# The scan's triangular inverse in 64x64 products, and four buffers zeroed a stage earlier

## The chip, the cores and the metric

The kernel runs on one core of a Trainium2 chip. The metric is the device time of one launch in microseconds (us), as the median of three runs. The engines are named as in the profile: PE is TensorE's matmul, PEld its weight load, DVE is VectorE, ACT is ScalarE, POOL is GpSimd, SP is SyncE.

## What is computed

A decoder layer on 512 tokens of width 1024: a projection, eight heads of RWKV-7 time mixing beside eight heads of dilated window attention, an output projection, and a feed-forward stage that picks single experts by product keys. The part that matters here is the recurrence of the time mixing, per head a state of 64x64:

```python
def step(state, inp):
    r_t, w_t, k_t, v_t, a_t, b_t = inp
    sa = jnp.einsum('bhij,bhj->bhi', state, a_t)
    state = (state * w_t[:, :, None, :] + sa[..., None] * b_t[:, :, None, :]
             + v_t[..., None] * k_t[:, :, None, :])
    return state, jnp.einsum('bhij,bhj->bhi', state, r_t)
...
_, y = lax.scan(step, state0, xs)
```

## The kernel before

The program is a chain of stages, each a block in which every engine runs its own instruction list: `project`, `attend`, `prepare`, `scan`, `normalise_heads`, `mix`, `route`, `experts`. The engines meet only through semaphores: `wait_ge` holds an engine's whole list, `then_inc` counts a finished instruction. Between stages there is a meeting of all engines, and GpSimd alone clears the semaphores of the stage that ended (`next_stage`, line 167). Nothing reorders the lists: the order is the one written.

`prepare` (line 524) computes the scaled vectors of all tokens. GpSimd has two instructions there: a small one at line 606, and at line 608 a product that waits for VectorE (`s_k`).

`scan` (line 691) works through the 512 tokens in 8 chunks of 64 (C = 64), in two halves of HC = 4 chunks. Two heads share the 128 partitions: partitions 0 to 63 hold the even head of a pair, 64 to 127 the odd one (`par`). There are HP = 4 pairs. Matrices of a pair lie in block-diagonal buffers `*_bd` of shape [128, 4 chunks, 4 pairs, 128], whose off-diagonal quarters are zero. In each half:

1. VectorE copies the scaled vectors into the diagonal blocks of `bbd` and `kbd` (lines 912 to 918). In the first half this waits for GpSimd's memsets (line 741; eight buffers, counted by `s_zero`).
2. Chunk by chunk TensorE forms Gram products (lines 775 and 778); VectorE masks them into `lbd`, `rbtbd`, `aktbd`, `rktbd` (line 929) and starts the inverse in `ttbd` (line 936); GpSimd adds the identity (line 745).
3. The triangular inverse, for the four chunks together, in NL = 5 levels (lines 794 to 829). It keeps an inverse T in `tbd` and its transpose in `ttbd`. A level is: X = L^T T for each chunk (TensorE, line 814), masked into `xbd` by VectorE (line 942); the "turn", a transpose of T through PSUM (line 799), copied out by ScalarE (line 890); then the second product, `ttbd` by `xbd` (line 827), added to T by VectorE (line 948). In the last level the order of the operands is swapped, so the result is the transpose. `xbd` and `ttbd` are the memory of `bbd` and `kbd`; `tbd` lies in `mixed`. The products with L of chunk c use PSUM bank c % 2, the second products bank 2 + c % 2, and the turns bank 4 + c, so a product waits for the evacuation of the one two chunks before (`s_xbd`, `s_yadd`).
4. Chunk after chunk, a chain through the state (lines 832 to 856), whose products are made by `two_heads` (lines 197 to 203): for each pair, two products with 64 of the 128 stationary columns each, into the two halves of the output partitions (line 202).

In the second half VectorE also runs `norm_step` (line 666) of the first half's output, one step after the second addition of each level (lines 949 and 950).

## Time and profile before

| | us |
|---|---|
| median of three runs | 1902.52 (1901.14 to 1902.91) |
| the profiled execution, as a whole | 1903.89 |
| its span | 1901.9 |
| scan, about | 288 to 484 of the span |
| inverse, first half | 325.5 to 373.1 |
| inverse, second half | 417.7 to 466.6 |

The profile is of one execution. Times are microseconds from the start of the span. A row of the timeline merges equal instructions that follow each other: start, time from the first's start to the last's end, engine, line, operation, output<-inputs, shape, count, and in brackets how long the engine was idle before and who ended that. An fp32 product is two matmul records and two weight-load records, a transpose one of each. The row "PEclk" and the clock in the windows give the granted clock as a share of 2.4 GHz; 0.50 is 1.2 GHz. Matmul records overlap, so the distance between two starts is the price of a group, and not its duration.

### The profile page before, as it was taken

How to read it: one execution, taken by the hardware profiler on the slowest of the kernel's cores; microseconds unless marked ns; L12 is line 12 of the kernel's file. 1: busy time of each engine (PE TensorE's matmuls, PEld its weight loads, DVE VectorE, ACT ScalarE, POOL GpSimd, SP SyncE). 2: the span in 40 equal slices, each digit the busy share in tenths (PEclk: the TensorE clock that was granted, in tenths of full speed). 3: DMA queues.
4: the chain of work that ended last, by engine and by line, in shares of the span. 5: the costliest groups of instructions: out<-in, count | busy, mean ns of one | idle time of the engine just before them, and what ended most of it. 6: DMA issues, size and time to landing. Idle time of an engine off the chain costs nothing.

```text
span 1901.9 us, 26134 instructions
## 1 busy us (share of the span) xinstructions
PE 1726.2 (91%) x9853; PEld 1512.0 (79%) x9853; DVE 1440.0 (76%) x2785; ACT 719.8 (38%) x1060; POOL 609.4 (32%) x356
## 2 busy tenths in 40 slices
PE   8998855979579887989998999999999999999997
PEld 6875325878468776979998999999999999978886
DVE  5564686566645999979994666888888888887765
ACT  4113542222232222358885333333333333333333
POOL 0000014010003546533333223656655655631100
PEclk9999987999799988989999999999999999999999
DMA  6310000000402223435657878999999999999983
GB/s 251 94 62 1 1 0 1 2 2 2 161 30 93 87 75 102 150 96 221 228 231 276 300 237 305 340 362 358 335 385 342 361 349 356 320 357 329 317 298 126
DMA packets 124284, 377.59 MB, mean 199 GB/s; under 512 B 11648, under 2 KB 49792, under 8 KB 123136
## 3 DMA queue, kind: packets, MB, share of 16 engines
q1 hardware_dynamic: 79664, 231.44, 34.1%
q0 software_dynamic: 36864, 134.23, 19.6%
q10 hardware_dynamic: 7632, 10.26, 1.5%
q8 instruction: 78, 1.28, 0.3%
q14 instruction: 46, 0.38, 0.1%
HBM read 338.40 MB, written 37.49 MB: 198 GB/s over the span
## 4 chain that ended last, share of the span: by engine, by line
PE 43%; DVE 11%; DMA 2%; ACT 1%; issue 0%; SPq 0%; DVEq 0%; ACTq 0%
PE ps L187 14%; PE ps L189 14%; PE ps L188 14%; DVE gated_cols L1724 8%; DVE onehot_rows L1727 2%; DMA hidden_ahead_tile<-hidden_ahead 1%; DMA wq_raw<-in_u_t 1%; ACT gate_stage L1634 0%; DVE h L1794 0%; DVE h L1801 0%; DVE v_lo L1777 0%; DVE h L1747 0%; ACT onehot_rows L1622 0%; PE ps L1828 0%; SPq L1540 0%
## 5 line engine op out<-in xcount | busy, mean ns | idle before, releaser
L187 PE MATMUL ps<-v_hi,a_hi 128*128 128x512 f32 x768 | 299.3, 390 | 2.9 <-DVE a_lo L1780 2.7
L189 PE MATMUL ps<-v_hi,a_lo 128*128 128x512 f32 x768 | 299.3, 390 | 0.0
L188 PE MATMUL ps<-v_lo,a_hi 128*128 128x512 f32 x768 | 298.8, 389 | 0.0
L187 PE MATMUL ps<-xn_hi,u_hi 128*128 128x384 f32 x832 | 282.8, 340 | 13.0 <-DVE u_lo L1716 8.5
L189 PE MATMUL ps<-xn_hi,u_lo 128*128 128x384 f32 x832 | 280.3, 337 | 0.0
L188 PE MATMUL ps<-xn_lo,u_hi 128*128 128x384 f32 x832 | 280.2, 337 | 0.0
L1606 POOL DMA_INDIRECT v_selected<-in_v,expert_index x128 | 186.2, 1454 | 290.5 <-DVE h L1747 277.4
L1777 DVE TENSOR_TENSOR v_lo<-v_raw,v_hi 128x1024 fp32r<-128x1024 f32 x128 | 156.7, 1224 | 114.1 <-ACT v_hi L1692 113.2
L1597 POOL DMA_INDIRECT u_selected<-in_u_rows,expert_index x128 | 180.9, 1413 | 141.7 <-DVE hidden_selected L1734 114.4
L1687 ACT ACTIVATE hidden<-ps 128x384 f32<-128x384 f32 x76 | 37.4, 492 | 397.5 <-PE ps L189 397.5
L1229 POOL TENSOR_TENSOR wq_lo<-wq_raw,wq_hi 128x1024 fp32r<-128x1024 f32 x40 | 102.5, 2567 | 259.0 <-ACT wq_hi L1270 259.0
L1692 ACT ACTIVATE v_hi<-v_raw 128x1024 fp32r<-128x1024 f32 x128 | 134.9, 1054 | 129.0 <-PE ps L189 117.4
L187 PEld LDWEIGHTS ps<-xn_hi,u_hi 128*128 128x128 f32 x832 | 157.9, 190 | 16.6 <-DVE u_lo L1716 8.8
L187 PEld LDWEIGHTS ps<-v_hi,a_hi 128*128 128x128 f32 x768 | 144.1, 188 | 31.8 <-DVE v_lo L1777 3.5
L1747 DVE SCALAR_TENSOR_TENSOR h<-v_selected,act_selected,h 128x1024 f32<-128x1024 f32 x128 | 163.9, 1280 | 7.0 <-DMA v_selected<-in_v,expert_index 2.9
L189 PEld LDWEIGHTS ps<-v_hi,a_lo 128*128 128x128 f32 x768 | 144.1, 188 | 30.2
L188 PEld LDWEIGHTS ps<-v_lo,a_hi 128*128 128x128 f32 x768 | 144.2, 188 | 26.8
L1734 DVE CUSTOM_DVE_ANT_0 dot_products<-u_selected,xn_tok 128x1024 bf16<-128x1024 f32 x128 | 153.8, 1220 | 14.4 <-DMA u_selected<-in_u_rows,expert_index 14.2
L188 PEld LDWEIGHTS ps<-xn_lo,u_hi 128*128 128x128 f32 x832 | 157.9, 190 | 3.4
L189 PEld LDWEIGHTS ps<-xn_hi,u_lo 128*128 128x128 f32 x832 | 157.6, 189 | 0.0
L1724 DVE TENSOR_SCALAR gated_cols<-consts_late,mixed 128x128 f32<-128x128 f32 x384 | 154.2, 473 | 0.0
L187 PE MATMUL ps<-xn_hi,wq_hi 128*128 128x384 f32 (+1 forms) x320 | 121.7, 380 | 35.3 <-POOL wq_lo L1229 35.2
(303 smaller groups left out, 3269.6 us busy)
## 6 DMA issues: line engine op xcount, KB each, us to landing
wq_raw<-in_u_t SPq DMA_DIRECT2D x128, 512.0 KB, 6.6
v_raw<-in_v SPq DMA_DIRECT2D x128, 512.0 KB, 6.6
gate_matrix<-gate_stage SPq DMA_DIRECT2D x6, 4096.0 KB, 13.0
gates<-gate_matrix SPq DMA_DIRECT2D x32, 768.0 KB, 8.3
win_raw<-in_win_t SPq DMA_DIRECT2D x26, 512.0 KB, 3.6
hidden_ahead_tile<-hidden_ahead SPq DMA_DIRECT2D x52, 192.0 KB, 5.9
wq_raw<-in_wq_t SPq DMA_DIRECT2D x16, 512.0 KB, 3.3
hidden_ahead<-hidden_ahead_tile ACTq DMA_DIRECT2D x28, 192.0 KB, 4.5
```

Source lines behind the costliest of these rows:

```text
L187: nc.tensor.matmul(out, w_hi, m_hi, start=first, stop=False)
L188: nc.tensor.matmul(out, w_hi, m_lo, start=False, stop=False)
L189: return nc.tensor.matmul(out, w_lo, m_hi, start=False, stop=last)
L1229: st.do(pool.tensor_tensor(w_lo[:, n % SPL, :], raw[:, n % RQ, :], w_hi[:, n % SPL, :].bitcast(F32), ALU.subtract), s_lo)
L1597: pool.indirect_dma_start(u_sel[:, i % GB, :], None, u_rows, bass.IndirectOffsetOnAxis(S.expert[:, i:i + 1], 0)).then_inc(s_usel[i % GB], 16)
L1606: pool.indirect_dma_start(v_sel[:, k % GB, :], None, v_rows, bass.IndirectOffsetOnAxis(S.expert[:, k:k + 1], 0)).then_inc(s_vsel[k % GB], 16)
L1692: act.activation(v_hi[:, n % 2, :], v_raw[:, n % VR, :], ACT.Copy).then_inc(s_vhi, 1)
L1724: v.tensor_scalar(cols[r % R][:, q, :], S.const("iota"), tab[:, 1, tok:tok + 1], tab[:, 2, tok:tok + 1], ALU.is_equal, ALU.mult).then_inc( ...
L1727: v.tensor_tensor(rows[r % R][:, :, :], bc(S.const("iota"), 1, Q), bc(tab[:, 0, r * Q:(r + 1) * Q], 2, NKEY), ALU.is_equal).then_inc(s_row ...
L1734: v.tensor_tensor_reduce(products[:, i % 2, :], u_sel[:, i % GB, :], S.xn_tok[:, :], 1.0, 0.0, ALU.mult, ALU.add, h_sel[:, i:i + 1]).then_ ...
L1747: v.scalar_tensor_tensor(S.h[:, GT, :], v_sel[:, k % GB, :], a_sel[:, k:k + 1], S.h[:, GT, :], ALU.mult, ALU.add).then_inc(s_sum, 1)
L1777: v.tensor_tensor(v_lo[:, p, :], v_raw[:, n % VR, :], v_hi[:, p, :].bitcast(F32), ALU.subtract).then_inc(s_vlo, 1)
```

## The change

In the inverse, T and X are kept compact, as `tc` and `xc` of [128, 4 chunks, 4 pairs, 64], both in the memory of `mixed`. Every product of a pair, the turns included, is made by the new `by_head`: for each pair and each of its two heads one product with a stationary operand of 128x64 and a moving operand of 128x64, into that head's 64 output partitions. The turn is now an ordinary product with 64 columns of the identity. The PSUM results fill 256 of a bank's 512 columns, so VectorE's masks and additions are 128x256 instead of 128x512. ScalarE writes a turned chunk into the diagonal blocks of `ttbd` with two instructions on 64 partitions (level 0: one compact copy of 128x256). In the last level VectorE writes X and adds the result block by block, two instructions each. The buffers `bbd`, `kbd`, `lbd` and `rbtbd` are allocated before `prepare`, and GpSimd zeroes them there, between its two instructions; four memsets stay in `scan`, and VectorE waits there for two of them.

```diff
@@ prepare, GpSimd
             st.do(pool.tensor_scalar(omka[:, :], S.param_all("k_a"), -1.0, 1.0, ALU.mult, ALU.add), s_pd)
+            for buf in (S.bbd, S.kbd, S.lbd, S.rbtbd):
+                st.do(pool.memset(buf[:, :, :, :], 0.0))
             pool.wait_ge(s_k, 1)
@@ scan
-        tbd = S.mixed[:, 0:4, :].rearrange("p c (j t) -> p c j t", j=HP)
+        tc, xc = (S.mixed[:, 2 * i:2 * i + 2, :].rearrange("p a (b j t) -> p (a b) j t", b=2, j=HP) for i in range(2))
+        def by_head(out, lhs, rhs):
+
+            for j in range(HP):
+                for e in range(2):
+                    last = nc.tensor.matmul(out[par[e], j, :], lhs(j, par[e]), rhs(j, par[e]), start=True, stop=True)
+            return last
@@ scan, GpSimd
-            for buf in (bbd, kbd, lbd, rbtbd, aktbd, rktbd, abd, rbd):
+            for buf in (aktbd, rktbd, abd, rbd):
                 st.do(pool.memset(buf[:, :, :, :], 0.0), s_zero)
@@ scan, TensorE
                     def turn(c, src):
-                        for j in range(HP):
-                            last = nc.tensor.transpose(blocks(4 + c)[:, j, :], src[:, c, j, :], S.const("ident"))
-                        last.then_inc(s_turn, 1)
+                        by_head(half_bank(4 + c), src, lambda j, h: S.const("ident")[:, h]).then_inc(s_turn, 1)
...
-                        for j in range(HP):
-                            last = nc.tensor.matmul(blocks(c % 2)[:, j, :], lbd[:, c, j, :], tbd[:, c, j, :],
-                                                    start=True, stop=True)
-                        last.then_inc(s_x, 1)
+                        by_head(half_bank(c % 2), lambda j, h: lbd[:, c, j, h], lambda j, h: tc[:, c, j, :]).then_inc(s_x, 1)
...
+                            by_head(half_bank(2 + c % 2), lambda j, h: ttbd[:, c, j, h],
+                                    lambda j, h: xc[:, c, j, :]).then_inc(s_y, 1)
@@ scan, ScalarE
-                        st.do(act.activation((ttbd if level else tbd)[:, c].rearrange(row), S.ps[:, 4 + c, :],
-                                             ACT.Copy), s_turned)
+                        turned = half_bank(4 + c)
+                        if level == 0:
+                            st.do(act.activation(tc[:, c], turned, ACT.Copy), s_turned)
+                            continue
+                        for e in range(2):
+                            st.do(act.activation(ttbd[par[e], c, :, par[e]], turned[par[e]], ACT.Copy), s_turned)
@@ scan, VectorE
                 for i, (dst, src) in enumerate(((bbd, S.bs), (kbd, S.ks))):
-                    if not half:
-                        dve.wait_ge(s_zero, i + 1)
...
+                        if level < NL - 1:
+                            st.do(v.tensor_tensor(xc[:, c], x, bc(mask, 1, HP), ALU.mult), s_xbd)
+                            continue
+                        for e in range(2):
+                            st.do(v.tensor_tensor(xbd[par[e], c, :, par[e]], x[par[e]], bc(mask[par[e]], 1, HP),
+                                                  ALU.mult), (None, s_xbd)[e])
...
+                        if level < NL - 1:
+                            st.do(v.tensor_tensor(tc[:, c], tc[:, c], y, ALU.add), s_yadd)
+                        else:
+                            for e in range(2):
+                                to = ttbd[par[e], c, :, par[e]]
+                                st.do(v.tensor_tensor(to, to, y[par[e]], ALU.add), (None, s_yadd)[e])
```

On TensorE, in the scan's first half, from the last Gram work (`kt_bd`) over the turns of level 0 into level 1. Before (`consts_late` is the identity, `mixed` holds T, `b_bd` X and `k_bd` the transpose of T):

```order
L202 MATMUL ps<-v_chunk,kt_bd 64x64 x8
L799 MATMUL ps<-consts_late,k_bd 128x128 x16
L814 MATMUL ps<-mixed,l_bd 128x128 x16
L827 MATMUL ps<-b_bd,k_bd 128x128 x16
L814 MATMUL ps<-mixed,l_bd 128x128 x16
L799 MATMUL ps<-consts_late,mixed 128x128 x16
```

And now, at the same place:

```order
L202 MATMUL ps<-v_chunk,kt_bd 64x64 x8
L740 MATMUL ps<-consts_late,k_bd 64x64 x32
L740 MATMUL ps<-mixed,l_bd 64x64 x32
L740 MATMUL ps<-mixed,k_bd 64x64 x32
L740 MATMUL ps<-mixed,l_bd 64x64 x32
L740 MATMUL ps<-consts_late,mixed 64x64 x32
```

The sequence is the same; each step has 32 small products instead of 16 large ones, and X is read from `mixed` instead of `b_bd`.

On ScalarE, around levels 0 to 2 of the first half, before:

```order
L890 ACTIVATE mixed<-ps 128x512 x4
L897 ACTIVATE a_bd<-r_and_a 64x16x64
L890 ACTIVATE k_bd<-ps 128x512 x4
L897 ACTIVATE a_bd<-r_and_a 64x16x64
L890 ACTIVATE k_bd<-ps 128x512 x4
```

And now:

```order
L895 ACTIVATE mixed<-ps 128x256 x4
L904 ACTIVATE a_bd<-r_and_a 64x16x64
L898 ACTIVATE k_bd<-ps 64x4x64 x8
L904 ACTIVATE a_bd<-r_and_a 64x16x64
L898 ACTIVATE k_bd<-ps 64x4x64 x8
```

From level 1 on, four copies of a turned chunk have become eight, each with a quarter of the elements.

On GpSimd, from the preparation's two instructions to the scan's last memset (`b_bd`, `k_bd`, `l_bd` and `rbt_bd` are the four buffers; the 20 ISA instructions clear semaphores):

```order
 L606 TENSOR_SCALAR one_minus_k_a<-params 128x4
-L608 TENSOR_TENSOR prepare_tmp<-z_mixed 128x2048
+L608 MEMSET b_bd 128x2048
+L608 MEMSET k_bd 128x2048
+L608 MEMSET l_bd 128x2048
+L608 MEMSET rbt_bd 128x2048
+L610 TENSOR_TENSOR prepare_tmp<-z_mixed 128x2048
 L527 UNCONDITIONAL_BRANCH
 L173 ISA x20
-L737 UNCONDITIONAL_BRANCH
-L741 MEMSET b_bd 128x2048
-L741 MEMSET k_bd 128x2048
```

Four memsets have moved from behind the 20 clearing instructions to before the preparation's product.

## Rows read from the trace of the kernel before

**Rows 1.** The page, its first line: the span.

```profile
span 1901.9 us, 26134 instructions
```

**Rows 2.** Windows: stretch, length, busy time by engine, TensorE's clock, DMA share, GB/s.

```profile
325.50:373.10 47.60, 46.85 (x400) 45.25 (x400) 27.59 (x40) 14.41 (x24) 0.00 (x0) 1.00 0.00 1
373.10:390.00 16.90, 11.96 (x320) 10.30 (x320) 8.82 (x25) 1.54 (x4) 0.00 (x0) 1.00 0.01 2
417.70:466.60 48.90, 46.92 (x400) 45.24 (x400) 31.73 (x47) 16.08 (x27) 1.99 (x1) 1.00 0.01 1
```

**Rows 3.** Timeline of one level of the inverse, first half.

```profile
334.91 3.95 PE L814 MATMUL ps<-mixed,l_bd 128*128 128x128 f32 x32
...
338.70 1.91 PE L799 MATMUL ps<-consts_late,mixed 128*128 128x128 f32 x16
...
340.45 3.95 PE L827 MATMUL ps<-b_bd,k_bd 128*128 128x128 f32 x32
...
341.54 0.69 DVE L948 TENSOR_TENSOR mixed<-mixed,ps 128x512 f32<-128x512 f32 x1 [1.95 <-PE ps L827]
...
344.24 3.95 PE L814 MATMUL ps<-mixed,l_bd 128*128 128x128 f32 x32
```

**Rows 4.** Timeline of TensorE: two groups of line 202 in a row.

```profile
308.59 0.64 PE L202 MATMUL ps<-v_chunk,rkt_bd 128*64 128x64 f32 x16
309.05 0.64 PE L202 MATMUL ps<-v_chunk,kt_bd 128*64 128x64 f32 x16
```

**Rows 5.** Timeline at the start of the chain behind the inverse.

```profile
373.16 0.69 PE L202 MATMUL ps<-z_mixed,a_bd 128*64 128x64 f32 x16 [0.78 <-DVE k_bd L948]
...
373.99 0.42 DVE L966 TENSOR_TENSOR z_mixed<-ps,v_products 128x256 f32<-128x256 f32 x1 [0.89 <-PE ps L202]
374.33 0.41 DVE L968 TENSOR_TENSOR z_mixed<-z_mixed,v_products 128x256 f32<-128x256 f32 x1
...
374.47 0.69 PE L202 MATMUL ps<-z_mixed,k_bd 128*64 128x64 f32 x16 [0.16 <-DVE z_mixed L966]
```

**Rows 6.** Timeline: VectorE and ScalarE with instructions of 256 columns.

```profile
304.42 0.87 DVE L929 TENSOR_TENSOR l_bd<-ps,consts 64x256 f32<-64x256 f32 x2 [3.66 <-PE ps L778]
...
309.74 0.94 ACT L868 ACTIVATE v_products<-ps 128x256 f32<-128x256 f32 x3 [0.70 <-PE ps L202]
```

**Rows 7.** Timeline: a step of the normalisation between two additions, second half.

```profile
426.08 1.22 DVE L673 TENSOR_REDUCE y_mean<-z_mixed 128x16 f32<-128x1024 f32 x1
```

**Rows 8.** Timeline from the preparation's end to TensorE's start; last, the second half's copies.

```profile
285.26 2.48 DVE L663 TENSOR_TENSOR z_mixed<-ps,z_mixed 128x512 f32<-128x512 f32 x4
289.81 1.80 POOL L741 MEMSET b_bd<- 128x2048 f32 x1 [13.44 <-issue]
...
291.65 4.54 DVE L916 COPY b_bd<-b_scaled 64x1024 f32<-64x1024 f32 x2 [3.90 <-POOL b_bd L741]
293.30 2.35 POOL L741 MEMSET l_bd<- 128x2048 f32 x1
...
300.82 2.08 PE L775 MATMUL ps<-r_and_a,b_bd 128*128 128x128 f32 x8 [18.87 <-DVE k_bd L916]
...
390.26 1.40 DVE L916 COPY b_bd<-b_scaled 64x1024 f32<-64x1024 f32 x2
```

**Rows 9.** Timeline: VectorE's first instruction of the stage behind the scan.

```profile
484.46 1.22 DVE L673 TENSOR_REDUCE y_mean<-z_mixed 128x16 f32<-128x1024 f32 x1 [0.32 <-PEq L695]
```

**Rows 10.** Timeline: two instructions of VectorE in the preparation.

```profile
245.39 0.43 DVE L625 TENSOR_SCALAR kk_inverse<-kk_inverse 128x512 f32<-128x512 f32 x1 [2.68 <-ACT kk_inverse L589]
...
260.74 1.22 DVE L634 TENSOR_TENSOR_SCAN decay_sum<-consts,decay_rate 128x512 f32<-128x512 f32 x1 [1.87 <-ACT gate L596]
```

**Rows 11.** Timeline of TensorE: the same groups at half the clock.

```profile
321.66 1.12 PE L202 MATMUL ps<-v_chunk,akt_bd 128*64 128x64 f32 x16 [2.91 <-DVE rkt_bd L929]
322.57 1.07 PE L202 MATMUL ps<-v_chunk,rkt_bd 128*64 128x64 f32 x16
323.43 1.07 PE L202 MATMUL ps<-v_chunk,kt_bd 128*64 128x64 f32 x16
```

More of the change, by code:

```diff
@@ L699, in scan @@
         HC = NCH // 2
-        bbd = sb("b_bd", [P, HC, HP, P])
-        kbd = sb("k_bd", [P, HC, HP, P])
+        bbd, kbd, lbd, rbtbd = S.bbd, S.kbd, S.lbd, S.rbtbd
         abd = sb("a_bd", [P, HC, HP, P])
@@ L731, in scan, with half_bank @@
         row = "p j t -> p (j t)"
-        def blocks(bank):
-            return S.ps[:, bank, :].rearrange("p (j t) -> p j t", j=HP)
+        def half_bank(bank):
+            return S.ps[:, bank, 0:HP * C].rearrange("p (j t) -> p j t", j=HP)
+        def by_head(out, lhs, rhs):
[3 more added lines that the diff above has]
+            return last
         @block.gpsimd
@@ L804, in _ @@
                             pe.wait_ge(s_eye, half * HC + c + 1)
-                            turn(c, ttbd)
+                            turn(c, lambda j, h: ttbd[:, c, j, h])
                     for c in range(HC):
                         if level == 0:
-                            pe.wait_ge(s_turned, n + c + 1)
+                            pe.wait_ge(s_turned, half * HC * (2 * NL - 1) + c + 1)
                         else:
@@ L884, in _ @@
                 take_products(half * HC + HC - 1)
-                act.wait_ge(s_zero, 9)
+                act.wait_ge(s_zero, 5)
                 spread_out = [(w, dst, e) for w, dst in ((0, abd), (1, rbd)) for e in range(2)]
@@ L925, in _ @@
                                                           (aktbd, g2, 0, "strict"), (rktbd, g2, 1, "inclusive"))):
-                        if not ch:
-                            dve.wait_ge(s_zero, 3 + i)
+                        if not ch and i >= 2:
+                            dve.wait_ge(s_zero, i - 1)
                         for e in range(2):
@@ L953, in _ @@
                 if not half:
-                    dve.wait_ge(s_zero, 9)
+                    dve.wait_ge(s_zero, 5)
                 dve.wait_ge(s_prev, 3 * HC * (half + 1))
@@ L1919, in build @@
                 S.ks = sr("k_scaled", [P, HP, T])
+                S.bbd, S.kbd, S.lbd, S.rbtbd = (sr(f"{name}_bd", [P, NCH // 2, HP, P]) for name in ("b", "k", "l", "rbt"))
                 prepare(nc, S, dram)
```

24 lines of the change are left out of this document (10 added, 14 removed).

## The prediction

> **What bounds the kernel now.** I read the windows first, then the timeline of one level of the inverse, then the timelines of the places where the same kinds of instruction already run in the new shape. The profiled span is 1901.9 us [rows 1]. The two inverses, one per half of the chunks, take 47.6 us and 48.9 us of it, together 5%; TensorE is busy for 46.85 and 46.92 us of them at a granted clock of 1.00 (2.4 GHz), while VectorE is busy for 27.59 and 31.73 us and ScalarE for 14.41 and 16.08 us [rows 2]. So in this stage TensorE is the bound. The timeline of one level shows it without a hole: products with L from 334.91, turns from 338.70, second products from 340.45, the next level's from 344.24, a period of 9.33 us, and VectorE waits for TensorE before its instructions [rows 3]. A level has 4 chunks of 4 pairs of heads. Each fp32 product of 128x128 by 128x128 is two records (32 for 16 products), so a record of a product costs (344.24 - 340.45) / 32 = 118 ns, and a turn, one record, (340.45 - 338.70) / 16 = 109 ns [rows 3]. Per chunk: 0.95 us for a product, 0.44 us for a turn. Only TensorE's cost per chunk, and then whatever comes next on VectorE and ScalarE, can move the time here. Everything after the scan stays as it is and only shifts.
>
> **The change part by part.** *The price of the new products.* Each product of a pair becomes two with a stationary operand of 64 columns and a moving operand of 64. Both still contract over all 128 partitions, because the operands taken from block-diagonal buffers hold zeros in the other head's half. That is exactly the shape in which line 202 already works: 16 records (8 products) for a chunk, alternating between the two halves of the output partitions. Of three such groups back to back the second starts at 308.59 and the third at 309.05, 0.46 later: 29 ns per record [rows 4]. The new group is therefore 0.46 us for a product instead of 0.95. A turn loses its one-record form and becomes 16 records as well: 0.46 instead of 0.44. A level's TensorE work falls from 9.33 to 12 x 0.464 = 5.57 us.
>
> *What is late next.* TensorE will not reach 5.57, since each product's PSUM bank is used again two chunks later. In the chain behind the inverse the same group starts at 373.16 and VectorE takes it at 373.99, 0.83 later; the 128x256 addition lasts 0.42 and the next group of TensorE starts at 374.47, 0.06 after its end; VectorE's own pitch is 0.34 (373.99 to 374.33) [rows 5]. So the third product of a level can't start before 0.83 + 0.42 + 0.05 = 1.30 us, where TensorE would be ready at 0.93: a wait of 0.37, once for the products with L and once for the second ones. Period: 5.57 + 2 x 0.37 = 6.31 us. ScalarE now takes a turned chunk with two 64-partition copies of 256 columns. The nearest row has three 128x256 copies in 0.94 us, a pitch of 0.28 [rows 6], so 0.56 per chunk; the first of four is out 1.5 us after its turn began (0.83 + 0.28 + 0.38), before TensorE is through its four turns (1.86), and the fourth at 3.2, when its product would start at 1.86 + 1.76 = 3.6. It stays hidden; at a pitch of 0.42, half as much again, it would cost up to 2 us in a half.
>
> *One half in sum.* Four turns 1.86; level 0, whose turns these are, 6.31 - 1.86 = 4.45; levels 1 to 3, 3 x 6.31 = 18.9. In the last level the results go block by block into block-diagonal buffers, two VectorE instructions of 64x256 at a pitch of 0.44 (two in 0.87 to 0.88) [rows 6]: a bank comes free 0.44 later, the four products take 3.08 instead of 2.23, and from the level's first product to its last addition it is 3.08 + 1.86 + 2.62 + 0.83 + 0.93 = 9.3. Sum 34.6 us. The same bookkeeping with 118 and 109 ns gives 47.5 for the kernel before, where the trace has 47.6 (325.5 to 373.1), so I trust it. Saving in the first half: 13.0.
>
> *The second half.* After the second addition of levels 0 to 3 VectorE also runs one step of the first half's normalisation, 1.22 us for the long ones plus a short one or two [rows 7]. Before, much of it lay beside TensorE's work. Now VectorE comes out of it about 0.8 us after the next product has landed (0.5 for the single-instruction steps), and the third product of the next level waits for it: 0.8 + 0.5 + 0.5 + 1.0 = 2.8. So 37.4 us against 48.8 in the trace: 11.4 saved. Together the inverses give 24.4.
>
> *The zeroing.* Four of the eight memsets leave the start of the scan. There VectorE is done with the preparation at 285.26 + 2.48 = 287.74, but its first copy starts at 291.65, when GpSimd's first memset (from 289.81) is done; and each of the four copies takes 2.27 beside the memsets (the first two 4.54 together), against 0.70 in the second half (two in 1.40). The memsets beside them last 2.35 instead of 1.80. TensorE starts at 300.82 [rows 8]. In the new code the copies wait for no memset of this stage. GpSimd's first one comes late because it clears 20 semaphores first; the others don't wait for that, for where the scan ends, VectorE goes from one stage's last instruction to the next stage's first with 0.32 us of idle time [rows 9]. So: copies at 288.06, two done at 289.46, the third in flight when the memset issues at 289.81 and done at 290.2, the fourth held until the memset ends (290.2 + 1.8 = 292.0) and done at 292.5. TensorE then starts at 292.6: 8.2 us earlier. Bounds: if VectorE does wait for the semaphores to be cleared, all four copies run beside memsets, 289.9 + 0.6 + 3 x 2.28 = 297.3, and 3.4 us are saved; if nothing collides, 288.06 + 2.8 = 290.9, 9.9 saved. I take 8.2, because the idle of 0.32 is the nearest row. The four memsets that stay end about 297.9; VectorE needs the first two of them at about 296.2.
>
> *The memsets' new place.* GpSimd does them from 239.4 to about 247, and its next work is not due until 269.9. On VectorE one instruction of that stretch is of the kind that could collide, the scaling at 245.39; the most is one memset, 1.8 us. Behind it VectorE waits 1.87 us before 260.74 for the last gate from ScalarE, whose chain doesn't pass through it, so a delay of that size is gone by then [rows 10]. I take nothing; with the cover gone it would be 1.8.
>
> Sum: 13.0 + 11.4 + 8.2 = 32.6 us. The profiled execution took 1903.89 us as a whole, 2.0 around its span, and lies 1.4 above the median of 1902.52; no term depends on that difference, so I take the sum off the median: **1870 us**.
>
> **Rivals.** (a) *The start of the scan gives little, the inverse all.* VectorE is held until the clearing is over, or the collisions are worse. The row of 0.32 us speaks against it, but that row stands at the scan's end and not its start. Saving 24.4 + 3.4 or less: 1875.
>
> (b) *TensorE's narrow records don't keep 29 ns, or ScalarE or VectorE paces.* The 29 ns come from 48 records in a row at most; a half now has 960 of them. At 33 ns the same bookkeeping gives 37.6 + 39.9 us, 5.6 more; slow strided writes on ScalarE and a VectorE pitch of 0.44 for the masks would add 2 to 3. Time 1876 to 1882.
>
> (c) *The clock falls.* After 2.91 us without work TensorE ran its groups at half the clock, 16 records in 0.86 us, 53 ns each (322.57 to 323.43) [rows 11]. If the new holes kept it there all through, both inverses would take 106.9 against 96.4: 10.5 lost, 8.2 gained, 1905, no change. Against it: in the chain behind the inverse TensorE is busy 11.96 of 16.90 us, with holes of 0.6 to 0.8, and the clock stays at 1.00 [rows 2, 5]; in the new inverse the holes are 0.4.
>
> (d) *Slower.* The 29 ns are a quarter of 118 for half the columns on both sides, so the two column halves must overlap in a burst. If in a long stream they run one behind the other, a record costs half of 118, 59 ns. Then both inverses take about 117.7 us, 21.3 more, and with 8.2 back the time is 1915. It decides from 51 ns per record on: there the loss in the inverse equals the 8.2. For it speaks that no row shows more than three such groups on end; against it, that the third group lasts 0.64 us as the second does [rows 4].
>
> The Trainium skill has a rule for such a case, in "TensorE: Matmul & The Clock Gate", section "Wait — 56ns, not 53.3ns?": when the sequencer decodes in software, it spends about 62 ns on a MATMUL, and this binds once the array's work is shorter. By that rule, 62 ns per record, the inverses would take 122.7 us and the kernel 1920. The 16 records in 0.46 us [rows 4] speak against it, so it adds nothing to the chance of (d).
>
> **How the numbers follow.** The forecast, 1870, with its own range of 1865 to 1874 (copies without collision give 1868, 27 ns per record 1867, small waits up to 1874): 0.56. (a) 0.15, (b) 0.15, (c) 0.04, (d) 0.04. More than forecast, below 1865, from shorter latencies: 0.06. The range takes in the forecast, (a) and most of (b): 1864 to 1882. A measurement of this kernel can tell about 0.2%, 3.8 us, from no change: faster 0.91, same 0.04, slower 0.05.
>
> **What would show it.** In the windows each inverse should be about 35 and 37 us long with the clock at 1.00; groups of 16 records in 0.46 us; VectorE's waits short; a level's period 6.3, in the second half about 6.9. The first copy of the scan should start some 0.3 us after the preparation's last instruction, and TensorE some 4.9 us after that instruction. The prediction is wrong if the narrow records cost more than 35 ns in a stream, if the turns' ScalarE copies have a pitch over 0.4, or if the copies at the start still take 2.27 each.

## The result and the profile after

The changed kernel takes **1869.49 us** (median of four runs, 1865.54 to 1869.96), the kernel before 1902.27 in the same session: ratio 0.9824, 95% interval 0.9807 to 0.9841, so 32.8 us faster. The forecast was 1870 with a range of 1864 to 1882. The profiled execution took 1865.54 as a whole:

```profile
span 1863.7 us, 28421 instructions
```

Its windows for the two inverses answer to [rows 2] (stretch, length, then busy time of TensorE, its weight loads, VectorE, ScalarE and GpSimd, TensorE's granted clock, DMA):

```profile
314.57:350.35 35.78, 31.79 (x960) 30.02 (x960) 20.25 (x48) 17.73 (x40) 0.00 (x0) 1.00 0.01 3
...
394.55:434.19 39.64, 34.11 (x961) 32.30 (x961) 24.40 (x56) 19.34 (x42) 2.61 (x1) 0.94 0.01 4
```

47.6 us have become 35.8, and 48.9 have become 39.6. TensorE is no longer busy without a hole (31.8 of 35.8 us), and in the second half it had a granted clock of 0.94. Of [rows 3], one level of the first half:

```profile
320.92 2.42 PE L740 MATMUL ps<-mixed,l_bd 128*64 128x64 f32 x64
...
323.14 2.07 PE L740 MATMUL ps<-consts_late,mixed 128*64 128x64 f32 x64
323.85 3.19 ACT L898 ACTIVATE k_bd<-ps 64x256 f32<-64x256 f32 x8 [5.82 <-PE ps L740]
325.01 2.81 PE L740 MATMUL ps<-mixed,k_bd 128*64 128x64 f32 x64
...
327.62 2.43 PE L740 MATMUL ps<-mixed,l_bd 128*64 128x64 f32 x64
```

The period is 6.70 us (forecast 6.31): products with L 2.22 (forecast 2.23), turns 1.87 for 64 records, 29 ns a record (1.86), second products 2.61 (2.23). The row between them explains the last: ScalarE's eight copies take 3.19 us, a pitch of (3.19 - 0.38) / 7 = 0.40. In the last level, where VectorE writes block by block, one sees TensorE wait for all three reasons in turn:

```profile
341.04 1.13 PE L740 MATMUL ps<-mixed,l_bd 128*64 128x64 f32 x32
...
342.77 0.69 PE L740 MATMUL ps<-mixed,l_bd 128*64 128x64 f32 x16 [0.59 <-DVE b_bd L953]
...
347.75 0.69 PE L740 MATMUL ps<-k_bd,b_bd 128*64 128x64 f32 x16 [0.52 <-ACT k_bd L898]
...
350.35 0.69 PE L202 MATMUL ps<-z_mixed,a_bd 128*64 128x64 f32 x16 [1.02 <-DVE k_bd L963]
```

A bank that VectorE has not freed (342.77), ScalarE's copy (347.75), and the last addition (350.35).

The start of the scan, answering to [rows 8]:

```profile
283.59 1.28 DVE L665 TENSOR_TENSOR z_mixed<-ps,z_mixed 128x512 f32<-128x512 f32 x2
285.18 1.41 DVE L921 COPY b_bd<-b_scaled 64x1024 f32<-64x1024 f32 x2 [0.32 <-PEq L527]
286.62 2.98 DVE L921 COPY k_bd<-k_scaled 64x1024 f32<-64x1024 f32 x2
286.93 2.12 POOL L747 MEMSET akt_bd<- 128x2048 f32 x1 [13.44 <-issue]
289.00 2.35 POOL L747 MEMSET rkt_bd<- 128x2048 f32 x1
289.65 2.08 PE L781 MATMUL ps<-r_and_a,b_bd 128*128 128x128 f32 x8 [9.40 <-DVE k_bd L921]
```

The copies begin 0.32 us after the preparation's last instruction (284.87) and TensorE 4.79 after it; before, 3.91 and 13.08. Three copies run alone and the fourth is held by the first memset, just as forecast.

The second half begins like this:

```profile
394.55 3.68 PE L740 MATMUL ps<-consts_late,k_bd 128*64 128x64 f32 x64 [1.03 <-ACT v_products L871]
...
402.35 1.22 DVE L675 TENSOR_REDUCE y_mean<-z_mixed 128x16 f32<-128x1024 f32 x1
402.95 1.13 PE L740 MATMUL ps<-mixed,l_bd 128*64 128x64 f32 x32
...
404.91 1.15 PE L740 MATMUL ps<-mixed,l_bd 128*64 128x64 f32 x32 [0.83 <-DVE mixed L950]
```

64 records of the turns take 3.68 us where the first half's take 2.08: here TensorE ran at half its clock. Further down VectorE's normalisation step (402.35) holds the third product at 404.91 by 0.83.

In the preparation the four memsets lie where they were meant to, and one instruction meets them:

```profile
243.25 1.79 POOL L608 MEMSET rbt_bd<- 128x2048 f32 x1
244.11 1.22 DVE L627 TENSOR_SCALAR kk_inverse<-kk_inverse 128x512 f32<-128x512 f32 x1 [2.68 <-ACT kk_inverse L589]
```

1.22 us in place of the 0.43 of [rows 10]. Of these 0.8 us 0.1 are left at the end of the preparation, as the next experiments show.

**The ledger of the profiled executions.** From the span's start to the second chain's first instruction it is 466.67 us before and 434.19 after. Stage by stage, each read as the distance between two starts in the timeline (us):

| stage | before | after | forecast saving | saving |
|---|---|---|---|---|
| ahead of the preparation | 238.45 | 237.17 | 0 | 1.28 |
| preparation | 49.29 | 47.69 | 0 | 1.60 |
| its end to TensorE's start | 13.08 | 4.79 | 8.2 | 8.29 |
| Gram stage, first half | 24.71 | 24.92 | 0 | -0.21 |
| inverse, first half | 47.63 | 35.78 | 13.0 | 11.85 |
| chain and Gram stage, second half | 44.62 | 44.20 | 0 | 0.42 |
| inverse, second half | 48.89 | 39.64 | 11.4 | 9.25 |
| everything behind | 1435.2 | 1429.5 | 0 | 5.7 |

The stages that the change touches give 8.29 + 11.85 + 9.25 = 29.4 of the forecast 32.6. The other 8.8 us of this pair of executions lie in stages on which the forecast put nothing; what the runs say of them follows.

### The profile page after: what moved, and what is told of

The parts are those of the page before. It is cut to its first block, busy times and chain, and to the rows that moved or that the text cites. A ratio compares the mean times of both kernels' runs of the same rounds, so it can differ in the third digit from the quotient of the medians.

```text
span 1863.7 us, 28421 instructions
## 1 busy us (share of the span) xinstructions
PE 1694.3 (91%) x10973; PEld 1481.2 (79%) x10973; DVE 1421.8 (76%) x2801; ACT 728.1 (39%) x1092; POOL 606.8 (33%) x356
## 4 chain that ended last, share of the span: by engine, by line
PE 45%; DVE 11%; DMA 1%; issue 0%; ACT 0%; POOL 0%; SPq 0%; DVEq 0%; ACTq 0%
PE ps L187 15%; PE ps L189 15%; PE ps L188 15%; DVE gated_cols L1739 8%; DVE onehot_rows L1742 2%; DMA gates<-gate_matrix 1%; DMA hidden_ahead_tile<-hidden_ahead 1%; PE ps L1843 0%; DVE h L1809 0%; DVE h L1816 0%; POOL u_lo L1605 0%; DVE v_lo L1792 0%; ACT v_hi L1707 0%; ACT u_hi L1632 0%; ACT o_ss L1673 0%
## 5 line engine op out<-in xcount | busy, mean ns | idle before, releaser
L1702 ACT ACTIVATE hidden<-ps 128x384 f32<-128x384 f32 x76 | 37.4, 492 | 380.0 <-PE ps L189 374.6
```

Of the source, the lines that this page charges most:

```text
L1702: act.activation(act_g[:, n % 2, :], S.ps[:, (NMID + n) % 2, 0:TD], ACT.Gelu).then_inc(s_gelu, 1)
```

## Experiments

All are edits of the changed kernel, but for the first, which is the kernel before with one part of the change. The two parts apart come first. A ratio is that to the kernel before in the same session; the changed kernel's is 0.9824 (0.9807 to 0.9841).

**e1: the zeroing alone.** The inverse stays in 128x128 products.

```diff
+            for buf in (S.bbd, S.kbd, S.lbd, S.rbtbd):      # in prepare, before wait_ge(s_k, 1)
+                st.do(pool.memset(buf[:, :, :, :], 0.0))
-            for buf in (bbd, kbd, lbd, rbtbd, aktbd, rktbd, abd, rbd):
+            for buf in (aktbd, rktbd, abd, rbd):
```

> The kernel before with one part of the change: the four buffers are allocated and zeroed in the preparation, the inverse stays in 128x128 products. Theory A (the parts act alone and add up): VectorE's first copy in the scan starts 0.3 us after the preparation's last instruction, TensorE about 4.8 us after it instead of 13.1; the time falls by 8.3 us, to 1894. Theory B (the 3 to 4 us of the gain that neither the inverse nor the scan's start shows in the trace belong to the move of the memsets, through the preparation's timing): the time falls by 11 to 12 us, and the preparation itself is 1.6 us shorter in the trace each time.

**e2: the inverse alone.** The eight memsets and their waits stay in the scan.

```diff
-            for buf in (S.bbd, S.kbd, S.lbd, S.rbtbd):
-                st.do(pool.memset(buf[:, :, :, :], 0.0))
-            for buf in (aktbd, rktbd, abd, rbd):
+            for buf in (bbd, kbd, lbd, rbtbd, aktbd, rktbd, abd, rbd):
```

> The changed kernel with all eight memsets in the scan again, and VectorE waiting for them; the inverse in 64x64 products. Theory A: the scan's start is as slow as before (TensorE 13.1 us after the preparation's last instruction), the inverses take 35.8 and 37.6 to 39.6 us, the time is 8.3 us above the changed kernel, about 1878. Theory B: 1881, and a preparation as long as in the kernel before (49.3 us).

Measured: e1 1894.13 us against 1901.28 (ratio 0.9958, 0.9942 to 0.9975), e2 1878.15 (0.9874, 0.9857 to 0.9890). So 7.2 and 23.1 us; together 30.3, against 32.8 for both at once, within the spread of some 2 us that each median has. In the trace of e1 TensorE starts 4.79 us after the preparation's end, in that of e2 13.08. Rival (a), a start that gives 3.4 or less, is out.

Of the preparation they tell more than of its memsets. It lasts 47.70 us in e1 and 47.69 in the changed kernel, both with the memsets; but also 47.58 in e2, without them, and 49.23 and 49.25 in e4 and e5 below, with them. So it has two lengths 1.6 us apart, and which one comes does not go by the memsets. It goes by TensorE's clock. In the five long ones (the kernel before, e4, e5, e7, e12) some products of the preparation ran at half clock after TensorE had waited 2.07 us, as here in the kernel before:

```profile
249.47 1.92 PE L567 MATMUL ps<-z_mixed,up_weights 128*128 128x512 f32 x2
```

In the eight short ones the same products ran at full clock behind the same wait (1.02 us at 248.16 in the changed kernel). The collision of 0.8 us costs 0.1, 47.69 against 47.58, and the 1.6 of the ledger are no saving of the change.

And e1 shows what the half clock is worth, in the old 128x128 shape, with not one instruction of the inverse changed. Its timeline at the first inverse's start:

```profile
312.24 0.69 PE L202 MATMUL ps<-v_chunk,akt_bd 128*64 128x64 f32 x16 [2.70 <-DVE rkt_bd L926]
312.75 0.64 PE L202 MATMUL ps<-v_chunk,rkt_bd 128*64 128x64 f32 x16
313.22 0.99 PE L202 MATMUL ps<-v_chunk,kt_bd 128*64 128x64 f32 x16
...
315.24 3.67 PE L798 MATMUL ps<-consts_late,k_bd 128*128 128x128 f32 x16 [1.03 <-ACT v_products L867]
```

The turns take 3.67 us where they took 1.97, and this inverse lasts 49.97 us against 47.63 before: 2.3 us from a clock that fell between two groups (0.64, then 0.99), after TensorE had waited 2.70 us.

**e3: half of ScalarE's copies.** Only the even heads' turned blocks are copied, so the odd heads' part of the inverse is left out; TensorE's and VectorE's instructions all stay.

```diff
-                        for e in range(2):
-                            st.do(act.activation(ttbd[par[e], c, :, par[e]], turned[par[e]], ACT.Copy), s_turned)
+                        st.do(act.activation(ttbd[par[0], c, :, par[0]], turned[par[0]], ACT.Copy), s_turned)
```

> The changed kernel with one of ScalarE's two copies of each turned chunk left out in levels 1 to 4 (the odd heads' blocks of the transposed inverse are not refreshed, so part of the output is not computed). Theory A (ScalarE's copies, 0.80 us per chunk, set when the second products may start, and cost 0.4 us per level): a level falls from 6.70 to 6.31 us, the first half's inverse from 35.8 to about 34.4. Theory C (the 0.4 us come from TensorE itself, narrow records with other operands being slower, or from VectorE): the level stays at 6.7.

Measured: 1866.45 us (one run). The level shows the cause:

```profile
331.90 1.78 ACT L896 ACTIVATE k_bd<-ps 64x256 f32<-64x256 f32 x4 [3.46 <-PE ps L740]
333.07 2.42 PE L740 MATMUL ps<-mixed,k_bd 128*64 128x64 f32 x64
```

The next level's products start at 335.29: with four copies the second products take 2.22 us, what the sum had (2.23), where with eight of them they take 2.61 (325.01 to 327.62). The level start to start is 6.32, where the changed kernel has 6.70 and the forecast 6.31. ScalarE's pace is the missing 0.4 us of a level. The first inverse as a whole took 37.17 us, since it began at half clock; for the same reason one can't read the gain from its length.

**e4: four banks.** Each chunk's products get a bank of their own (PSUM banks 0 to 3 for both kinds), and the two waits for VectorE two chunks back go.

```diff
-                        if n + c >= 2:
-                            pe.wait_ge(s_xbd, n + c - 1)
-                        by_head(half_bank(c % 2), lambda j, h: lbd[:, c, j, h], lambda j, h: tc[:, c, j, :]).then_inc(s_x, 1)
+                        by_head(half_bank(c), lambda j, h: lbd[:, c, j, h], lambda j, h: tc[:, c, j, :]).then_inc(s_x, 1)
```

> The changed kernel with four PSUM banks instead of two for each kind of product: chunk c uses bank c for the product with L and again for the second one, so no product waits for the evacuation two chunks before. Theory A (bank waits of 0.37 us stand once in the products with L, and the second products are paced by ScalarE): the products with L take 1.86 us instead of 2.22, the second ones stay near 2.6, a level takes 6.35 instead of 6.70, the last level gains another 0.5 to 1, the time falls by 3 to 4 us against the changed kernel. Theory C (TensorE's own pace for the stream is the limit): no change.

Measured: 1865.44 us (0.9809, 0.9792 to 0.9826). Timeline of a level of the first half:

```profile
330.64 2.09 PE L740 MATMUL ps<-mixed,l_bd 128*64 128x64 f32 x64
...
332.51 2.09 PE L740 MATMUL ps<-consts_late,mixed 128*64 128x64 f32 x64
333.23 3.20 ACT L894 ACTIVATE k_bd<-ps 64x256 f32<-64x256 f32 x8 [2.20 <-PE ps L740]
334.38 2.89 PE L740 MATMUL ps<-mixed,k_bd 128*64 128x64 f32 x64
...
337.06 1.16 PE L740 MATMUL ps<-mixed,l_bd 128*64 128x64 f32 x33
```

Products with L now take 1.87 us, no more than the turns, so the bank wait was worth 0.35 (forecast 0.37). The second products still take 2.68: there two waits lie over each other, the bank's and ScalarE's, and ScalarE's ends last. So taking the bank's away alone gives nothing there, while e3, which took ScalarE's away, gave 0.39 and left the bank's. The second half's inverse falls most, to 34.06 us against 37.75 at full clock with two banks (e11). Its levels 2 and 3 take 6.40, as in the first half, since VectorE's normalisation steps then no longer hold a bank that TensorE wants; level 1 still takes 7.04. The median can't be told from the changed kernel's.

**e5: the scan's memsets held back** until VectorE's first four copies are done.

```diff
+            pool.wait_ge(s_bd, 4)
             for buf in (aktbd, rktbd, abd, rbd):
```

> The changed kernel; GpSimd starts the scan's four memsets only when VectorE's four copies are done. Theory A (a copy that meets a memset waits for it, nothing else slows the copies): all four copies take 0.71 us, TensorE starts 3.2 us after the preparation's last instruction instead of 4.8, the time falls by 1.6 us against the changed kernel, to 1868. Theory D (the copies' wait is hidden, since VectorE later waits for the held memsets instead): TensorE starts earlier, but the first turn of the first half does not.

Measured: 1867.07 us (0.9809, 0.9794 to 0.9824). The timeline:

```profile
287.80 1.41 DVE L922 COPY b_bd<-b_scaled 64x1024 f32<-64x1024 f32 x2 [0.32 <-PEq L527]
289.24 1.41 DVE L922 COPY k_bd<-k_scaled 64x1024 f32<-64x1024 f32 x2
290.70 0.58 PE L782 MATMUL ps<-r_and_a,b_bd 128*128 128x128 f32 x1 [7.78 <-DVE k_bd L922]
290.71 1.80 POOL L748 MEMSET akt_bd<- 128x2048 f32 x1 [14.60 <-DVE k_bd L922]
```

Each of the four copies takes 0.70, the memset waits, and TensorE starts 3.22 us after the preparation's end in place of 4.79. So the held fourth copy was worth 1.57 us, what the sum put on it (292.5 against 290.9). In the median that cannot be told from nothing.

**e6: the normalisation step ahead of the level's additions**, where VectorE waits for ScalarE and TensorE anyway.

```diff
-                        if half and c == 1 and level < NL - 1:
-                            norm_step(S, dve, v, st, level, 0)
+                    if half and level < NL - 1:       # before the loop of the additions
+                        norm_step(S, dve, v, st, level, 0)
```

> The changed kernel; the normalisation step of levels 0 to 3 of the second half stands before the first addition of the level, where VectorE waits 1.9 us for TensorE, instead of after the second. Theory A (the steps delay the masks and with them the third product of the next level): the levels of the second half become as long as those of the first, 6.7 us instead of 7.4, 7.0 and 6.8, the second inverse is 1.8 us shorter, the time 1868. Theory C (the second half is longer only because TensorE started it at the half clock): the levels keep their length.

Measured: 1867.70 us (0.9822, 0.9806 to 0.9839). Start to start levels 1 to 3 of the second half are 6.71, 6.87 and 6.70 us, where the changed kernel has 7.40, 7.02 and 6.75, and the last level 9.31 in place of 10.07: 1.65 us won. But level 0 has no copies to wait for, so there the step only delays the additions, and turns and level 0 take 9.58 in place of 8.40. Of 1.65 us 0.47 stay, and the time can't be told from the changed kernel's. (e12 has four banks as well.)

**e7: Gram evictions by half of the partitions.** VectorE writes the four blocks of the even heads and then the four of the odd heads, in place of both halves of each buffer in turn. The same eight instructions.

```diff
-                    for i, (dst, src, w, m) in enumerate(outs):
-                        for e in range(2):
+                    for e in range(2):
+                        for i, (dst, src, w, m) in enumerate(outs):
```

> The changed kernel; VectorE writes the Gram products of a chunk first for the even heads (four instructions on partitions 0 to 63) and then for the odd ones, instead of alternating. Theory E (two instructions in a row on different halves of the partitions don't overlap, hence the pitch of 0.45 us against 0.34 for those on all partitions): within a group the pitch falls to 0.34, a chunk takes 3.9 us instead of 4.5, unless TensorE is then the bound at 4.2; the time falls by 2 to 5 us. Theory F (any instruction on 64 partitions, or with this access pattern, has this pitch): no change.

Measured: 1863.04 us (0.9792, 0.9777 to 0.9807).

```profile
295.46 0.42 DVE L935 TENSOR_TENSOR l_bd<-ps,consts 64x256 f32<-64x256 f32 x1 [3.88 <-PE ps L784]
295.80 0.41 DVE L935 TENSOR_TENSOR rbt_bd<-ps,consts 64x256 f32<-64x256 f32 x1
296.13 0.40 DVE L935 TENSOR_TENSOR akt_bd<-ps,consts 64x256 f32<-64x256 f32 x1
296.46 0.41 DVE L935 TENSOR_TENSOR rkt_bd<-ps,consts 64x256 f32<-64x256 f32 x1
296.90 0.43 DVE L935 TENSOR_TENSOR l_bd<-ps,consts 64x256 f32<-64x256 f32 x1
```

The first four starts are 0.34, 0.33 and 0.33 apart; the fifth, where the half changes, 0.44. In the order of before every step changed the half, at 0.45 each. A chunk takes 3.8 us in place of 4.5, the Gram stage 21.5 in place of 24.9, of which 1.2 are the clock (e11 below: 23.7 with the old order at full clock). And in both halves the inverse began at full clock. The expectation had 2 to 5 us for all this; the medians lie 6.4 apart, across two sessions.

**e10: ScalarE's two copies in alternating order.** If a change of the half costs VectorE 0.1 us, it may cost ScalarE as much.

```diff
-                        for e in range(2):
+                        for e in (1, 0) if c % 2 else (0, 1):
```

> The changed kernel with one edit: ScalarE's two copies of a turned block (one for the even heads, to partitions 0 to 63, one for the odd heads, to partitions 64 to 127) come in the order even, odd for chunks 0 and 2 and odd, even for chunks 1 and 3. So three of the seven steps from one copy to the next stay within one half of the partitions; before, all seven changed the half. Theory: the pitch of 0.40 us belongs to steps that change the half, as on VectorE, where steps within a half took 0.33 to 0.34 and steps between halves 0.44 when only its order was changed. Then steps within a half take 0.28 to 0.30, the eight copies 2.85 us in place of 3.19, the second products of a level 2.3 in place of 2.6, and a level start to start 6.4 in place of 6.7; four levels of two halves give 2 to 3 us, 1867 at most. Rival: 0.40 us is what any copy of 64 partitions takes on ScalarE when the copies come from four PSUM banks; then all pitches stay at 0.40 and the time is that of the changed kernel, 1869.

Measured: 1865.66 us (0.9817, 0.9800 to 0.9833).

```profile
328.66 2.43 PE L740 MATMUL ps<-mixed,l_bd 128*64 128x64 f32 x64
...
331.59 2.80 ACT L898 ACTIVATE k_bd<-ps 64x256 f32<-64x256 f32 x8 [2.44 <-PE ps L740]
...
334.97 2.43 PE L740 MATMUL ps<-mixed,l_bd 128*64 128x64 f32 x64
```

Eight copies take 2.80 us in place of 3.19. With 0.40 for the four steps that change the half, the other three are (2.80 - 0.38 - 1.60) / 3 = 0.27, which is the 0.28 that the forecast had taken from full-width copies. The level start to start is 6.31 us, the forecast's number. The second half gains less, 37.22 us against the 37.75 of e11, both begun at full clock, because there the normalisation steps hold TensorE. In time the gain, some 1.6 us, can't be told from the changed kernel; the trace carries the verdict.

**e11: work in TensorE's wait.** Ten products whose result nobody uses.

```diff
+                for _ in range(10):
+                    nc.tensor.matmul(S.ps[:, 0, 0:P], bbd[:, HC - 1, 0, :], S.const("ident"), start=True, stop=True)
                 products(half * HC + HC - 1)
```

> The changed kernel with one edit: ahead of the last chunk's products in each half, where TensorE waits 2.8 to 2.9 us for VectorE's eviction of rkt_bd, it runs ten 128x128 float32 products into a PSUM bank that is free there; their result is used by nothing. They take 2.4 to 2.6 us at full clock, so nothing is later. Theory: the wait is what drops the granted clock, and the half clock at the start of the inverse (64 turns in 3.68 us in place of 2.08) is its consequence; with the wait filled the turns of both halves take about 2.0, both inverses are 35 to 37.5 us, and the time falls by about 2 us for each half that was cold, to 1864 to 1868. Rival: the clock falls for another reason (a schedule of the chip that is not tied to this wait); then one or both inverses still begin at half clock and the time stays at 1869, or rises by what the products delay, if they outlast the wait.

Measured: 1869.12 us (1863.98 to 1872.65; 0.9828, 0.9807 to 0.9849).

```profile
309.23 2.50 PE L798 MATMUL ps<-consts_late,b_bd 128*128 128x128 f32 x20
...
311.96 0.69 PE L202 MATMUL ps<-v_chunk,akt_bd 128*64 128x64 f32 x16 [0.23 <-DVE rkt_bd L936]
...
314.61 2.08 PE L740 MATMUL ps<-consts_late,k_bd 128*64 128x64 f32 x64 [1.03 <-ACT v_products L873]
```

Both inverses begin at full clock, the second as well (turns 2.09 us), and last 35.78 and 37.75. The start of an inverse in all thirteen profiles:

| TensorE's wait ahead of the last chunk's products | cases | what the clock did |
|---|---|---|
| 2.91 or 2.92 us (both halves of before, one of after, e1, e2, e4, e6) | 7 | half at once: products in groups of 1.12, 1.07, 1.07; full again for the turns |
| 2.58 to 2.88 (one half of after, e1 to e4, e6, e10, both of e5) | 9 | first group still 0.69, then half; turns 3.67 or 3.68 |
| 2.20 and 2.27 (one half of e3 and e10) | 2 | stays |
| 0.2 to 1.2 (e7, e9, e11, e12) | 8 | stays |

So the clock falls after this wait nearly always, in the kernel before too, and what varies is where the slow stretch lies. On the products it costs 1.2 us (from their start to the turns 3.86 in place of 2.65), on the turns and level 0 2.3 to 2.7 (0.2 to 0.5 ahead of the turns, 2.0 to 2.4 behind). With the wait filled, the scan up to the second chain is 2.9 us shorter than in the changed kernel's profile, counted from the preparation's start (194.11 against 197.02): 3.8 won at the two starts, 0.9 lost in the chain between them.

That loss is again the clock, at a place where the changed kernel kept it:

```profile
350.39 0.94 PE L202 MATMUL ps<-z_mixed,a_bd 128*64 128x64 f32 x16 [1.02 <-DVE k_bd L965]
```

This group and the next three take 0.94, 1.07, 1.11 and 0.90 us (0.69, 0.64, 0.69 and 0.69 in the changed kernel), after a wait of only 1.02. Of the 26 chain starts behind an inverse six were like this: both of e9 and of e11, one of e4 and one of e7, after waits of 1.02 to 2.26 us; twenty others after waits of 0.78 to 1.52, thirteen of them of the same 1.02, were not. So the long wait is one thing after which the clock falls and not the only one, and filling it does not keep the clock up everywhere. What else decides is not shown.

The median did not follow: 1869.12 is outside the 1864 to 1868 that were expected. Everything behind the second inverse lasted 1435.8 us in this profile against 1429.5, of which the second chain's slow start is 0.5.

**e9 and e12: all of it together.** e9 is e4, e5, e6 and e7 in one, and VectorE takes two of a level's eight copies (the odd heads of chunks 0 and 1) in the time in which it waits for ScalarE.

```diff
+                    for c in range(2 if level else 0):       # VectorE, before the additions
+                        dve.wait_ge(s_turn, n + c + 1)
+                        st.do(v.tensor_copy(ttbd[par[1], c, :, par[1]], half_bank(4 + c)[par[1]]), s_td)
```

> The changed kernel with the four edits together: four banks, memsets held, normalisation in the gap, Gram products written by half; and VectorE copies the odd heads' blocks of the first two turned chunks in levels 1 to 4, so that ScalarE has six copies per level instead of eight. Theory A: a level takes 5.6 to 5.8 us in both halves, TensorE being the bound again, the inverses take 30 to 31 us with TensorE at full clock, the start gives 1.6: about 10 us less than the changed kernel, 1859. Theory C: TensorE can't keep 29 ns per record without pauses, or VectorE, now busy for most of the level, becomes the bound, and the level stays above 6.2: 1864.

Measured: 1852.88 us (0.9746, 0.9733 to 0.9760), inverses of 32.01 and 32.74 us, levels of 5.74. That is 6 us below the expected 1859, though the inverses are longer than the expected 30 to 31: the expectation put nothing on the Gram evictions by half, which in e7 had shortened the two Gram stretches by 3.4 and 2.1 us. The last level was still 9.13 (331.65 to 340.78):

```profile
332.35 3.60 DVE L953 TENSOR_TENSOR b_bd<-ps,consts 64x256 f32<-64x256 f32 x8
...
335.87 0.76 DVE L957 COPY k_bd<-ps 64x256 f32<-64x256 f32 x2
336.44 2.08 PE L741 MATMUL ps<-k_bd,b_bd 128*64 128x64 f32 x64 [0.83 <-ACT k_bd L897]
```

There VectorE's two copies come behind its eight masks, and TensorE waits for them (the row names ScalarE, whose copy of that chunk was long done; the group starts 0.15 us behind the end of VectorE's first copy, 335.87 + 0.42). e12 leaves the last level's copies to ScalarE and alternates the order of the halves on both engines:

```diff
-                    for c in range(2 if level else 0):
+                    for c in range(2 if 0 < level < NL - 1 else 0):
...
-                        for e in range(2):
+                        for k, e in enumerate((1, 0) if c % 2 else (0, 1)):    # last masks and additions
```

> The kernel of e9 (four product banks, the scan's memsets held until the first copies are done, the norm step ahead of the additions, Gram evictions by half of the partitions, two of eight copies of a level on VectorE) with two edits: in the last level ScalarE takes all eight copies again, since VectorE's two came behind its eight masks and held TensorE for 0.83 us; and wherever two successive instructions write the two halves of the partitions in turn, the order alternates so that half of the steps stay within one half (ScalarE's copies, VectorE's last masks and additions). Theory: the last level goes from 9.1 us to about 8.0, VectorE's 16 last instructions from a pitch of 0.45 to one of 0.39, twice; about 2 us in all, 1850.5. Rival: the second products of the last level wait for ScalarE's seventh and eighth copy instead, then nothing is won, 1853.

Measured: **1848.46 us** (1845.14 to 1851.55; 0.9718, 0.9702 to 0.9734), the fastest of all.

```profile
336.15 2.08 PE L741 MATMUL ps<-mixed,l_bd 128*64 128x64 f32 x64
336.86 3.24 DVE L959 TENSOR_TENSOR b_bd<-ps,consts 64x256 f32<-64x256 f32 x8
...
338.73 2.80 ACT L903 ACTIVATE k_bd<-ps 64x256 f32<-64x256 f32 x8 [2.13 <-PE ps L741]
...
343.88 0.69 PE L202 MATMUL ps<-z_mixed,a_bd 128*64 128x64 f32 x16 [1.52 <-DVE k_bd L974]
```

Eight of VectorE's instructions now take 3.24 us in place of 3.60, and the last level 7.73 in place of 9.13. The three levels ahead of it are 5.60 or 5.61, three groups of 1.87: TensorE is the bound again, at 29 ns a record.

**What the same code did in different executions.** The part behind the second inverse, in which no kernel here differs from another, lasted 1429.5 us in the changed kernel's profile, 1435.2 in that of before, and between 1431.8 and 1435.8 in the other eleven. That is where 5.7 of the 38.2 us between the two spans come from. Nothing of it lies in code that the change touches, and it is a reason that gains of 1 or 2 us are read from the traces here and not from the medians. Why it varies stays open.

## Why the prediction was right, and where it was not

**The price of the products: right.** 29 ns a record over the 960 records of an inverse: turns in 1.87 us for 64, as [rows 4] had them for 16. This takes away rival (d), 59 ns a record. The Trainium skill's figure beside it is about 62 ns for a MATMUL when the sequencer decodes in software ("TensorE: Matmul & The Clock Gate", section "Wait — 56ns, not 53.3ns?"). By it 64 records would take 4.0 us, an estimate, where the trace has 1.87; no run here shows which way the instructions were decoded.

**What is late next: half right.** Piece by piece, for the first half: turns 1.92 us (forecast 1.86), level 0 4.43 (4.45), levels 1 to 3 6.70 each (6.31), the last level 9.31 (9.3); 35.78 in all against 34.6. Everything but one term stands. The failed step is "The nearest row has three 128x256 copies in 0.94 us, a pitch of 0.28": the pitch measured is 0.40 when the copies go to the two halves of the partitions in turn, and then ScalarE, "hidden" in the forecast, paces the second products. e3 shows it by taking copies away, e10 by their order alone. The full-width row of [rows 6] was not the nearest one. The trace of before has the very shape, in the stage behind the scan, a pitch of (1.59 - 0.38) / 3 = 0.40:

```profile
485.12 1.59 ACT L1025 ACTIVATE mixed<-ps 64x256 f32<-64x256 f32 x4 [3.18 <-PE ps L1036]
```

For VectorE the forecast did look up the 64-partition shape and took 0.44, and there it was right. The bound "at a pitch of 0.42 [...] up to 2 us in a half" held: 1.2 us. This is the ScalarE part of rival (b); its other parts, slower records and masks at 0.44, did not come.

**The second half: 2.2 us too short, and at full clock right within 0.2, from two errors.** At half clock, turns and level 0 took 8.40 us (394.55 to 402.95) in place of 6.35, a 2.05 that the forecast had not; without them 39.64 is 37.6, against 37.4. ScalarE's copies account for 1.2 of it, so the normalisation steps cost less than the 2.8 of the forecast: 37.6 - 35.8 = 1.8, since part of a step lies under the longer wait for ScalarE. Where that wait is shorter, levels 1 to 4 of the second half are longer than those of the first by 2.4 (e3) and 2.6 us (e10), near the forecast's 2.8.

**The clock: the rival had the wrong place.** Rival (c) asked whether the new holes inside the inverse would keep the clock down, and they did not: 1.00 over the first inverse. What was missed is that the slow stretch after the wait of 2.91 us in [rows 11] can as well lie on the inverse itself. It belongs to no edit: e1 has it in the old shape. The argument against the rival, that holes of 0.6 to 0.8 us in the chain leave the clock at 1.00, held for the kernel before; behind waits of 1.02 us three of sixteen chain starts ran at half clock (e7, e11).

**The start of the scan: right.** 8.29 us for 8.2, with the copies at +0.32 and TensorE at +4.79 (forecast 0.3 and 4.9); the order of events, the held fourth copy included, is as written. The row of 0.32 at another stage's start [rows 9] was a good guide.

**The zeroing in the preparation: right in size, with a cover that is not always there.** The scaling was hit (0.43 to 1.22 us), and 0.1 us of that is left. But the idle of 1.87 us in [rows 10] that was to absorb it belongs to a preparation in which TensorE had run at half clock (249.47). At full clock and without the memsets (e2) VectorE is idle there for 0.59, and in the changed kernel not at all.

**The total: right, with some luck.** By stages the change gives 29.4 us in the profiled pair, 31.4 had the second half begun at full clock; the medians give 32.8, and those of the two parts apart 30.3. The forecast of 32.6 was 1.2 too high in each half by the copies, which in the second half the normalisation steps, priced 1.0 too high, gave back almost whole. That the median still falls on it is within the variation of the code that did not change.

## What to carry to other kernels

When an operation is cut into pieces on half of the partitions, look for a row with exactly that shape on each engine that touches it, in any stage of the program, and order the pieces so that neighbours stay in the same half. When the bound engine gets twice as fast, list the time of its helpers (bank reuse, evictions, copies) at the same granularity: here the next limit was two of them at the same place, and taking away the one that ended first showed nothing. A stage a few per cent of the program long is better judged by its own starts in the trace than by the median of the whole.

## What the runs showed of the hardware

- VectorE and ScalarE need more time from one instruction on 64 partitions to the next when the half of the partitions changes: VectorE 0.44 to 0.45 us against 0.33 to 0.34 (64x256, from PSUM), ScalarE 0.40 against 0.27. Order alone moves it (e7, e10, e12).
- Of a copy on VectorE and a memset on GpSimd one holds the other: copies of 0.70 us took 2.27 beside memsets, one that began just ahead of a memset ran through and the next waited for its end, and a memset took 2.12 to 2.35 in place of 1.80. A scaling of 0.43 took 1.22.
- Ahead of the last chunk's products, after waits of 2.58 to 2.92 us, TensorE's clock fell to 1.2 GHz in 16 of 16 cases, in 9 of them only after work had begun again (0.69, 0.64, then 0.99 us for equal groups in e1). It was back at 2.4 GHz within the inverse's level 0 at the latest. At other places it fell after shorter waits, but not each time: 2.07 us in the preparation (5 of 13 profiles), 1.02 behind an inverse (3 of 16).
- One preparation with the same work took 47.7 or 49.3 us, by whether that slow stretch came.
- fp32 products of 128x64 by 128x64, on the two halves of the output in turn, cost 29 ns a record, a quarter of the 118 ns of 128x128 by 128x128, over three groups of 64 records on end (e12). Which of the two, the smaller operands or the turn of the halves, gives how much no run separates.
